# Two begun output tiles instead of three in the recurrent mixer; another order of tiles, Silus and norms in the hybrid mixer

## What is computed

```python
proj = h @ w_in                      # q_a, kv_a, k_pe, z (512), xbc (1024), dt (8)
q, k, v = up-projections of normed q_a, kv_a; q and k normed per head, part of each turned by rope
attn_out = causal_attention(q, k, v)             # 8 heads
xbc = silu(causal_conv4(xbc) + conv_b)           # xs (512), B (256), C (256)
dt = softplus(dt_raw + dt_bias)
y = ssd_chunked(xs, dt, a, B, C) + d_skip * xs   # 4 chunks of 128 tokens
yg = group_rmsnorm(y * silu(z)) * ssd_norm_w
out = concatenate([attn_out, yg]) @ w_out
```

## Time and profile before

| | |
|---|---|
| median of 3 runs | 3392.42 us (3392.41 to 3394.08) |
| the profiled execution | 3393.59 us, its span 3391.9 us |
| TensorE busy | 3298.8 us, 97% of the span |
| VectorE, ScalarE, GpSimd busy | 1777.3 us (52%), 1153.4 us (34%), 75.7 us (2%) |
| chain that ended last | TensorE 89%, VectorE 6%, ScalarE 4% |
| the end of the recurrent mixer | about 1600 to 1690 us |
| the two hybrid mixers | about 2125 to 2378 us and 2760 to 3012 us |

### The profile page before, as it was taken

One profiled execution on the slowest core, in us unless ns is written; L12 is line 12 of the kernel. 1 busy time (PEld: TensorE's weight loads), 2 busy tenths in 40 slices (PEclk: granted clock), 3 DMA queues, 4 the chain that ended last, 5 costly groups with the idle time before them and its releaser, 6 DMA issues.

```text
span 3391.9 us, 37019 instructions
## 1 busy us (share of the span) xinstructions
PE 3298.8 (97%) x15359; PEld 2732.1 (81%) x15359; DVE 1777.3 (52%) x2519; ACT 1153.4 (34%) x1595; POOL 75.7 (2%) x100
## 2 busy tenths in 40 slices
PE   7999999999999999999899999999999999999999
PEld 6888876888888888888688887878788888878887
DVE  5664366566446664366466545775433347553332
ACT  4322253322233222362332223553322235432221
POOL 1000000000000000000000001100000010000000
PEclk9999999999999999999899999999999999999999
DMA  5443321344333443322144332211222322023322
GB/s 152 137 147 118 106 75 62 126 147 138 114 112 114 137 138 125 98 76 75 63 148 149 131 106 83 84 38 38 87 98 87 101 73 85 3 75 100 99 94 69
DMA packets 334141, 339.85 MB, mean 100 GB/s; under 512 B 12182, under 2 KB 329048, under 8 KB 333976
## 3 DMA queue, kind: packets, MB, share of 16 engines
q1 hardware_dynamic: 332696, 333.98, 30.4%
q0 software_dynamic: 1280, 3.50, 0.4%
HBM read 335.36 MB, written 2.10 MB: 99 GB/s over the span
## 4 chain that ended last, share of the span: by engine, by line
PE 89%; DVE 6%; ACT 4%; issue 1%; DMA 0%; POOL 0%; SPq 0%; DVEq 0%; POOLq 0%; ACTq 0%
PE ps L135 88%; DVE ar L100 1%; ACT ar L95 1%; DVE ar L108 1%; PE ps L138 1%; DVE wl L100 1%; ACT L95 1%; ACT wh L95 1%; ACT ch L95 1%; DVE ar L117 0%; DMA raw<-in_ffn_w 0%; DVE x L100 0%; DVE hl L108 0%; DVE ar L104 0%; DVE cl L100 0%
## 5 line engine op out<-in xcount | busy, mean ns | idle before, releaser
L135 PE MATMUL ps<-hh,wl 128*128 128x512 f32 x2760 | 1090.5, 395 | 20.9 <-DVE hl L108 15.3
L100 DVE TENSOR_TENSOR wl<-raw,wh 128x1024 fp32r<-128x1024 f32 (+2 forms) x547 | 655.2, 1200 | 811.1 <-ACT wh L95 810.6
L135 PE MATMUL ps<-hl,wh 128*128 128x512 f32 x2760 | 1079.9, 391 | 0.0
L135 PE MATMUL ps<-hh,wh 128*128 128x512 f32 x2760 | 1079.5, 391 | 0.0
L95 ACT ACTIVATE wh<-raw 128x1024 fp32r<-128x1024 f32 (+2 forms) x547 | 560.3, 1027 | 494.6 <-PE ps L135 480.3
L135 PEld LDWEIGHTS ps<-hh,wl 128*128 128x128 f32 x2760 | 522.0, 189 | 134.7 <-issue 28.0
L135 PEld LDWEIGHTS ps<-hh,wh 128*128 128x128 f32 x2760 | 521.7, 189 | 110.1
L135 PEld LDWEIGHTS ps<-hl,wh 128*128 128x128 f32 x2760 | 522.2, 189 | 105.4 <-issue 0.2
L135 PE MATMUL ps<-uh,wl 128*128 128x512 f32 x1056 | 411.8, 390 | 0.0
L135 PE MATMUL ps<-uh,wh 128*128 128x512 f32 x1056 | 410.9, 389 | 0.0
L135 PE MATMUL ps<-ul,wh 128*128 128x512 f32 x1056 | 410.8, 389 | 0.0
(11 more groups left out here) (217 smaller groups left out, 2696.0 us busy)
## 6 DMA issues: line engine op xcount, KB each, us to landing
raw<-in_ffn_w SPq DMA_DIRECT2D x120, 1024.0 KB, 5.1
raw<-in_w_ada SPq DMA_DIRECT2D x48, 1024.0 KB, 5.2
raw<-in_w_gate_up SPq DMA_DIRECT2D x44, 1024.0 KB, 5.0
raw<-in_m_w_in SPq DMA_DIRECT2D x26, 1024.0 KB, 5.5
raw<-in_w_down SPq DMA_DIRECT2D x16, 1024.0 KB, 5.2
raw<-in_ffn_w SPq DMA_DIRECT2D x16, 768.0 KB, 4.4
raw<-in_w_in SPq DMA_DIRECT2D x12, 1024.0 KB, 5.4
raw<-in_m_w_out SPq DMA_DIRECT2D x8, 1024.0 KB, 5.2
```

Of the source, the lines that this page charges most:

```text
L100: return self.issue(lambda e: e.tensor_tensor(out, a, b, op))
L135: return self.issue(lambda e: e.matmul(out, l, r, start=start, stop=stop, skip_group_check=True))
```

## The change

In `mix1`, `begin` takes output tiles 0 and 1 instead of 0, 1 and 2. In `mix2` the order of the tiles becomes z 0, z 1, xb 2, `heads_turned(0)`, xb 3, then in the loop xb 4, xb 5, xb 6, xb 7, z 2, z 3. ScalarE's three Silus of 128x2048 become one block that stands with z 3: both of xb behind the wait for the last convolution, then the copy of z 3, then that of z. On VectorE each convolution is made one product later than its tile; `normed` is cut in two (rope part `normed`, the rest `normed_nope`), of which the first comes with xb 7 and the second with z 2; the instructions for dt come with z 3; and `xd` is no longer made inside `turned` but in `decayed(t)`, three of them a step later and the fourth behind the copies of `gm`. Weights are loaded in the new order, in as many chunks of the same size.

```diff
-BETWEEN = [2, 3, 4, 5, 6, 7]
+BETWEEN = [("xb", 4), ("xb", 5), ("xb", 6), ("xb", 7), ("z", 2), ("z", 3)]
...
-                wide(st, ("z",), W, 416, 512)
+                wide(st, ("z",), W, 416, 256)
                 wide(st, ("xb",), W, 1184, 768, 2)
+                wide(st, ("z",), W, 672, 256, 2)
```

In `mix1` (so in TensorE's program; ScalarE's and VectorE's have the same line without the last three arguments):

```diff
-                begin(s, [("out", t) for t in range(3)], ch, cl, (s, "c"))
+                begin(s, [("out", 0), ("out", 1)], ch, cl, (s, "c"))
```

ScalarE in `mix2`:

```diff
-                    act.wait_ge(worked, (s, "conv", 7))
-                    act.f(A(20, 4), A(20, 4), ACT.Silu).then_inc(curved, (s, "xb", 1))
                     act.wait_ge(worked, (s, "de"))
...
-                        convolved(t)
-                    if t == 5:
-                        act.wait_ge(worked, (s, "conv", 3))
-                        act.f(A(16, 4), A(16, 4), ACT.Silu).then_inc(curved, (s, "xb", 0))
-
-                gate(2)
+                        act.wait_ge(worked, (s, "conv", 7))
+                        for i in range(2):
+                            act.f(A(16 + 4 * i, 4), A(16 + 4 * i, 4), ACT.Silu).then_inc(curved, (s, "xb", i))
+                        gate(3)
+                        act.own()
+                        act.f(A(24, 4), A(24, 4), ACT.Silu).then_inc(curved, (s, "z"))
+
+                convolved(2)
                 heads_turned(0)
-                gate(3)
-                act.own()
-                act.f(A(24, 4), A(24, 4), ACT.Silu).then_inc(curved, (s, "z"))
+                convolved(3)
```

VectorE in `mix2`:

```diff
+                def normed_nope(sd):
+                    q, kn = by_head(Qt, 96, sd)[:, :, :, 0:64], by_head(Kt, 64, sd)
+                    dve.wait_ge(worked, (s, "rs", sd))
+                    dve.tt(q, q, stats(rs, sd, 1).unsqueeze(3).to_broadcast([128, 4, 4, 64]), MUL).then_inc(worked, (s, "qn", sd))
+                    dve.tt(kn, kn, stats(rs, sd, 0).unsqueeze(3).to_broadcast([128, 4, 4, 64]), MUL).then_inc(worked, (s, "qkn", sd))
...
                     turned(3)
+                    for t in range(3):
+                        decayed(t)
                     yield 1
...
+                    decayed(3)
...
+                    product(s, *name)
+                    i = BETWEEN.index(name)
+                    if i < 5:
+                        conv_from(3 + i)
+                    if i == 3:
                         normed(1)
-                    if t == 3:
+                    if i == 4:
+                        normed_nope(1)
+                    if i == 5:
                         dve.wait_ge(curved, (s, "dln"))
...
                 heads_turned(0)
-                product(s, "z", 3)
+                conv_from(2)
+                product(s, "xb", 3)
```

More of the change, by code:

```diff
@@ L355, in h_end @@
         def h_end(s):
-            names = {"ffn": ("w3", 21), "ffn2": ("w3", 21), "mix0": ("xg", 3), "mix1": ("g", 7), "ple": ("gate", 7), "mix2": ("xb", 7)}
+            names = {"ffn": ("w3", 21), "ffn2": ("w3", 21), "mix0": ("xg", 3), "mix1": ("g", 7), "ple": ("gate", 7), "mix2": ("z", 3)}
             return G_of[(s, *names[s[0]])]
@@ L1113, in between @@
                 def between():
-                    t = next(fill, None)
-                    if t:
-                        product(s, ("xb", t), hh, hl, h)
+                    name = next(fill, None)
+                    if name:
+                        product(s, name, hh, hl, h)
                     else:
                         next(ssd, 0)
-                product(s, ("z", 2), hh, hl, h)
+                product(s, ("xb", 2), hh, hl, h)
                 heads_turned(0)
-                product(s, ("z", 3), hh, hl, h)
+                product(s, ("xb", 3), hh, hl, h)
                 for hd in range(10):
@@ L1570, in mix1 @@
                 turn(6, 7)
-                begin(s, [("out", t) for t in range(3)])
+                begin(s, [("out", 0), ("out", 1)])
                 out_product(s, nxt, True)
@@ L1769, in between @@
                 def between():
-                    t = next(fill, None)
-                    if t is None:
+                    name = next(fill, None)
+                    if name is None:
                         next(ssd, 0)
-                    else:
-                        convolved(t)
-                    if t == 5:
-                        act.wait_ge(worked, (s, "conv", 3))
-                        act.f(A(16, 4), A(16, 4), ACT.Silu).then_inc(curved, (s, "xb", 0))
-                gate(2)
+                    elif name[0] == "xb":
+                        convolved(name[1])
+                    elif name == ("z", 2):
+                        gate(2)
+                    else:
+                        act.wait_ge(worked, (s, "conv", 7))
[5 more added lines that the diff above has]
+                convolved(2)
                 heads_turned(0)
-                gate(3)
-                act.own()
-                act.f(A(24, 4), A(24, 4), ACT.Silu).then_inc(curved, (s, "z"))
+                convolved(3)
                 for hd in range(10):
@@ L2534, in mix2 @@
                 normed(0)
+                normed_nope(0)
                 product(s, "z", 1)
                 sums(1)
-                product(s, "z", 2)
+                product(s, "xb", 2)
                 def PT(hd, k):
@@ L2592, in turned, with decayed @@
                                TKt[:, 0, :, 2 * t:2 * t + 2].unsqueeze(3).to_broadcast([128, 4, 2, 64]), MUL).then_inc(left(k), k)
-                        dve.own()
+                    def decayed(t):
+                        heads4 = "p b (h n) -> p b h n"
+                        c = slice(128 * t, 128 * t + 128)
+                        dve.wait_ge(*left_of((s, "xt", t)))
                         dve.wait_ge(curved, (s, "de"))
-                        dve.tt(xd4[:, :, 128 * t:128 * t + 128].rearrange("p b (h n) -> p b h n", h=2), o,
+                        dve.tt(xd4[:, :, c].rearrange(heads4, h=2), xt[:, :, c].rearrange(heads4, h=2),
                                de[:, :, 2 * t:2 * t + 2].unsqueeze(3).to_broadcast([128, 4, 2, 64]), MUL).then_inc(worked, (s, "xd", t))
@@ L2691, in between @@
                 def between():
-                    t = next(fill, None)
-                    if t is None:
+                    name = next(fill, None)
+                    if name is None:
                         next(ssd, 0)
-                    else:
-                        convolved(t)
-                    if t == 2:
+                        return
+                    product(s, *name)
[3 more added lines that the diff above has]
+                    if i == 3:
                         normed(1)
-                    if t == 3:
+                    if i == 4:
+                        normed_nope(1)
+                    if i == 5:
                         dve.wait_ge(curved, (s, "dln"))
```

16 lines of the change are left out of this document (6 added, 10 removed).

## The result

The changed kernel takes 3366.9 us (median of 4 runs, 3365.6 to 3367.6), the kernel before 3392.4 us (3391.4 to 3394.1): ratio 0.9924, 95% interval 0.9908 to 0.9940. That is 25.5 us less; the forecast was 23.5 less, 3369 us. The profiled execution took 3367.2 us, its span is 3365.5. It stands 0.3 us above its median, that of before 1.2 us above its own.

The account below looks back on a forecast made before the run. TensorE, 89% of the chain of waits, was taken as the bound, so only its waits and lower clock could be won. 16.0 + (5.1 - 0.5) + (3.4 - 0.5) = 23.5 us off 3392.4 gave 3369 us, range 3360 to 3380.

Parts of the forecast that it names:

- Part 1: Recurrence: two begun tiles win 17.4 us, or 16.0 us with a clock fall behind the remaining 1.60 us wait.
- Part 2: Hybrid mixers, `turn(0)`: earlier minima of `scores(1)` remove TensorE's wait for ScalarE, winning 5.1 us and 3.4 us.
- (d): Mixers: four fewer table loads, no Silu starting `states()`: zero; clock fall behind dt stays: zero, at best 1.7 us each.
- (a): Mixers, VectorE: the moved rope part of `normed(1)`, 3.5 us, delays the minima of `scores(2)`, but stays hidden.
- (c): Mixers, VectorE: `normed_nope(1)` ends at 2240.2, needed for `heads_turned(4)` at 2246.4.
- (b): Mixers, block of Silus before dt's transposes: hidden with 0.7 us to spare; each us later costs TensorE 1 us, twice.
- (e): Mixers: `decayed(3)` between the copy of `gm` and the states product loses 0.5 us in each layer.
- (f): GpSimd's zeros of `T3[0]` and SyncE's sends of the same chunks: zero, about 5 us spare.
- only the recurrence gives: Rival: in the mixers another engine, the block above all, takes back 4.6 and 2.9 us; 3376.4 us, chance 0.15.
- The clock favours it: Rival: no clock fall behind the 1.60 us wait (1.4 us) or behind dt (1.7 each); 3364 us, chance 0.15.

Follow-up runs that it names:

- Experiment 6: The changed kernel with both halves of `normed(1)` put behind the convolution of xb 3: ratio 0.9921, 3366.4 us.
- experiment 5: The changed kernel with two more Copies of 128x1536 in ScalarE's block of Silus, ahead of `gate(3)`: ratio 0.9952, 3377.1 us.
- the run with dt late: The kernel before, with VectorE's three dt instructions and its scan behind the convolution of xb 7 instead of xb 3: ratio 1.0016, 3398.8 us.

## Why the prediction was right

- **Part 1, the recurrence.** The mechanism and the sum held: 17.4 us without a clock fall were worked out, 17.3 measured. What failed is the choice for the clock: I took 16.0, leaning to a fall behind the 1.60 us wait, and none came in any trace with two begun tiles. The ground for it was weak: in the trace of before the fall of 10.2 us began at 1620.7, and the wait of 5.25 us had begun at 1620.3, so the low mean clock from 1620.3 on told of the stretch of the second wait, which the change takes away, and not of the first. (The 1.4 us set down for a fall were also less than the 1.7 that the prediction had put as its price.) That the fall stayed out is seen; what decides it no run shows.
- **Part 2, the wait in `turn(0)`.** Gone in both mixers. 4.6 and 2.9 us net were forecast, 6.3 and 3.0 measured. The 1.7 us of the first are the fall behind dt that stayed out, the "at best" of (d).
- **(a), (c).** The rope part took 3.4 us (forecast 3.5), the minima of `scores(2)` started at 2212.93, 0.9 us behind the last of the scores' matmuls (forecast 1), and nothing waited. Experiment 6 shows that there was room for the whole norm.
- **(b), the block.** Forecast cover 0.7 us, measured 0.55. Two errors met in it: with the mixer's 16.8 us earlier start taken off, convolution 7 ended 0.6 us later than worked out (2221.64), and from there to the scan's end it took 0.3 us less. The step that was mis-sized is the price, "each us later costs 1 us": in experiment 5 it was 5.3 us in one mixer and 2.9 in the other for 2.3 us that dt's transposes came later. On the drain that the Trainium skill ("ScalarE: Activation LUTs", "What ACT_TABLE_LOAD costs") adds to a switch, the trace decides as before: in the run with dt late the load of 1.28 us ends at 2254.86 and the Silu starts at 2254.87. In the block of the changed kernel the load is hidden, since it ends at 2221.24 and the Silu waits until 2221.67 for the convolution.
- **(d), "nothing waits for them on TensorE, zero".** Right as a term, and luck as an argument: the prediction gave no worth to the two moves of which the first mixer's gain needs one. The Silu at the start of `states()` had no cover left before the change, and its stall on VectorE (2.94 us) was in the trace unread. Had the change left both that Silu and `xd` in place, 7 us would have been lost again (3366.9 to 3373.9). That is nearly the loss of the rival "only the recurrence gives" (7.5 us), though at another place than the block.
- **(e), `decayed(3)`.** 0.5 us each forecast, 0.55 measured, of which the row shows 0.38 as a wait. Moving `xd` was needed only as the second of two guards.
- **(f), GpSimd and SyncE.** Right: no new wait of TensorE names either.
- **The rivals.** "The clock favours it" came true in two of its three terms: no fall behind the 1.60 us wait, none behind dt in mixer 1, but one in mixer 2. The measured 3366.9 lies between the forecast of 3369 and its 3364. The others did not come true. The number of the first, 3376.4, is what two begun tiles alone give (3377.5).

The two errors that count, 1.4 us of the recurrence and 1.7 of mixer 1, are the same: clock falls that were expected and stayed out.

## What to carry to other kernels

Before a wait is taken away, follow the engine that it held up through the next stage, and look at the idle rows of the other engines there: a stall that costs nothing now can be the next wait, and, as here at 2260.4, half a clock may be what hides it. Give an engine that runs in order the work that frees banks first, and the work that waits for another engine last: then a late Exp stops one stream and not two. And ask what holds the buffers before reordering their fills: two begun tiles instead of three gave 17.3 us where an earlier split of the third gave 3.7.

## What the runs showed of the hardware

- A short wait of TensorE can cost several times its length, or only itself. Behind a wait of 1.90 us the granted clock was 0.50 for 10.3 us; waits of 2.62 us made one mixer 5.3 us longer and the other 2.9; behind the 1.6 us in the recurrence it stayed at 1.00 in all seven traces that have two begun tiles and this wait. So a range for such a term has to hold both.
- The same stages, with the same instructions and the same waits, differ by up to 2.5 us between kernels that changed nothing in them: from the end of mixer 1 to mixer 2 it is 370.1 to 372.6 us in these traces, with clock falls at the stage borders. That is as much as a small edit is worth, and only the stage with the edit in it can tell.
